# A decoder step on Trainium2: the RWKV triangular solve in 64-column diagonal blocks, merged with its preparation, without padded operands

## What is computed

```python
def step(s, inp):                       # s: value x key, 64 x 64
    rt, wt, kt, vt, kkt, at = inp
    sa = jnp.einsum('bhvk,bhk->bhv', s, -kkt)
    s = (s * wt[:, :, None, :] + sa[..., None] * (kkt * at)[:, :, None, :]
         + vt[..., None] * kt[:, :, None, :])
    return s, jnp.einsum('bhvk,bhk->bhv', s, rt)
```

## Time and profile before

| what | value |
|---|---|
| median of 3 runs | 1461.94 us (1459.42 to 1464.79) |
| the profiled execution: its time / its span | 1466.44 us / 1464.6 us |
| TensorE busy | 1351.8 us (92%) |
| VectorE / ScalarE / GpSimd busy | 972.0 / 646.6 / 395.0 us |
| mean granted TensorE clock | 0.951 of full speed |

### The profile page before, as it was taken

The page is one execution under the profiler, slowest core; times in us unless marked ns, Lnnn a source line. Parts: engine busy times, 40 slices in busy tenths (PEclk is TensorE's granted clock), DMA queues, the critical chain, the costliest instruction groups (busy, mean ns, idle before and its releaser), DMA issues.

```text
span 1464.6 us, 24455 instructions
## 1 busy us (share of the span) xinstructions
PE 1351.8 (92%) x8950; PEld 1177.1 (80%) x8950; DVE 972.0 (66%) x1820; ACT 646.6 (44%) x1492; POOL 395.0 (27%) x316
## 2 busy tenths in 40 slices
PE   6999865898879699999999999999999999799997
PEld 5988642687644499999999999999998778688886
DVE  4566689643543432999802777777776778688887
ACT  4432124332010345444455656656655555455554
POOL 1020113001010003879876000000014777222220
PEclk9999666999969899999999999999999999999999
DMA  6431110000032343555455444344346899889993
GB/s 227 136 115 58 65 74 2 1 2 30 2 126 88 119 128 108 161 150 158 146 171 152 127 130 127 123 130 129 123 136 208 286 300 314 296 300 310 309 320 103
DMA packets 117615, 219.32 MB, mean 150 GB/s; under 512 B 31648, under 2 KB 32160, under 8 KB 116512
## 3 DMA queue, kind: packets, MB, share of 16 engines
q1 hardware_dynamic: 87840, 180.58, 36.8%
q0 software_dynamic: 11264, 33.60, 7.6%
q10 hardware_dynamic: 18432, 4.20, 1.3%
HBM read 207.64 MB, written 10.42 MB: 149 GB/s over the span
## 4 chain that ended last, share of the span: by engine, by line
PE 53%; DMA 5%; POOL 3%; DVE 2%; ACT 2%; issue 1%; SPq 0%; ACTq 0%
PE ph L1720 10%; PE ph L1721 10%; PE ph L1722 10%; PE acc L1787 6%; PE acc L1789 6%; PE acc L1788 6%; PE pg L1768 4%; DMA raw<-in_v 3%; POOL lo L1593 3%; ACT hi L1623 1%; DVE lo L1802 1%; DMA raw<-in_uT 1%; DMA raw<-in_w_q 1%; DMA hid<-in_v 1%; PE acc L1740 1%
## 5 line engine op out<-in xcount | busy, mean ns | idle before, releaser
L1720 PE MATMUL ph<-xh,hi 128*128 128x320 f32 x1152 | 363.7, 316 | 9.5 <-DVE lo L1802 7.0
L1721 PE MATMUL ph<-xl,hi 128*128 128x320 f32 x1152 | 356.5, 309 | 0.0
L1722 PE MATMUL ph<-xh,lo 128*128 128x320 f32 x1152 | 356.4, 309 | 0.0
L1802 DVE TENSOR_TENSOR lo<-raw,hi 128x512 fp32r<-128x512 f32 x328 | 220.2, 690 | 143.9 <-ACT hi L1623 140.5
L1623 ACT ACTIVATE hi<-raw 128x512 fp32r<-128x512 f32 x456 | 268.7, 628 | 100.0 <-DMA raw<-in_uT 33.6
L1720 PEld LDWEIGHTS ph<-xh,hi 128*128 128x128 f32 x1152 | 217.0, 188 | 13.4 <-DVE lo L1802 7.3
L1721 PEld LDWEIGHTS ph<-xl,hi 128*128 128x128 f32 x1152 | 217.1, 188 | 0.0
L1722 PEld LDWEIGHTS ph<-xh,lo 128*128 128x128 f32 x1152 | 216.7, 188 | 0.0
L1593 POOL TENSOR_TENSOR lo<-raw,hi 128x512 fp32r<-128x512 f32 x128 | 186.7, 1482 | 103.5 <-ACT hi L1623 102.8
L1787 PE MATMUL acc<-hi,ch 128*128 128x512 f32 x512 | 201.4, 393 | 12.3 <-DVE cl L1937 12.1
L1788 PE MATMUL acc<-hi,cl 128*128 128x512 f32 x512 | 200.3, 391 | 0.0
(11 more groups left out here) (362 smaller groups left out, 1981.3 us busy)
## 6 DMA issues: line engine op xcount, KB each, us to landing
raw<-in_uT SPq DMA_DIRECT2D x256, 256.0 KB, 2.9
raw<-in_v SPq DMA_DIRECT2D x168, 256.0 KB, 4.3
hid<-in_v SPq DMA_DIRECT2D x88, 256.0 KB, 5.2
wraw<-in_w_in SPq DMA_DIRECT2D x30, 512.0 KB, 3.3
raw<-in_w_q SPq DMA_DIRECT2D x32, 256.0 KB, 3.0
wo<-in_w_out SPq DMA_DIRECT2D x4, 1024.0 KB, 10.8
h_scratch<-act_s ACTq DMA_DIRECT2D x128, 32.0 KB, 1.5
sth<-in_state_h SPq DMA_DIRECT2D x1, 2048.0 KB, 7.7
```

The source lines that it names most:

```text
L1720: pe.matmul(o, hi[s][:, k], xh[:, c], start=begin, stop=False)
L1721: pe.matmul(o, hi[s][:, k], xl[:, c], start=False, stop=False)
L1722: ins = pe.matmul(o, lo[s][:, k], xh[:, c], start=False, stop=end)
L1802: dve.tensor_tensor(wide(lo[n % RING]), raw_at(n)[0], wide(hi[n % RING]), ALU.subtract).then_inc(lo_v, 1)
```

## The change

- The preparation and the solve become one block. Bonus and the transposes of `Bh` and `Kh`, which stood in the preparation, are placed between solve steps on TensorE, ScalarE and VectorE. Their exponential goes to a tensor of its own, `kx`.
- `ARx` becomes `AR` with two parts, A and r times decay; a product for one head reads 64 rows. Nothing is zeroed in the preparation and GpSimd has no instruction in it: the `r` product goes to VectorE, the shift copies to ScalarE. The low-rank products of line 770 read 64 rows each.
- Tiles 0 and 1 keep only the diagonal blocks: all matrices are 128 x 8 x 64, the first chunk of a tile in rows 0 to 63 and the second in rows 64 to 127. Scores are products of 64 rows and 64 columns, four quadrants in turn, with one PSUM bank for each row group. A solve step is 16 products, both chunks in one bank. The masks are packed to this form.
- The three tiles advance together: step s of tile 0, of tile 1, and step s - 2 of tile 2. PSUM is a ring of six banks.
- In the recurrence operands are 64 rows; the state `st` holds both heads of a pair side by side with zeros between, so that four products of 128 rows replace eight; parts that need no state are issued ahead; the sample states are read in 64-row products, scaled by 32 ScalarE instructions, and V is spread for all heads at the start of the block by GpSimd.

Its core, with new functions; masks and additions of the other tiles follow the same pattern, and `y_local`, `s_local`, `u_all`, `s_new`, `y_new` are eight products of 64 rows each, `y_state` four of 128, `carried` one of 512 columns:

```diff
-(M_ID, M_BU, M_BL, M_EU, M_SU, M_IU, M_TBU, M_TBL, M_TIU, M_HI, M_HO, M_B64) = range(NMASK)
+NMASK = 10
+(M_ID, M_BB, M_ES, M_II, M_TBU, M_TBL, M_TIU, M_HI, M_HO, M_B64) = range(NMASK)
...
+    row, left = s % 64, t < 64
+    side = t % 64
+    near = row // 16 == side // 16
+    m[:, M_BB] = near & np.where(left, row < side, row > side)
+    m[:, M_ES] = (row < side) & (~near | ~left)
+    m[:, M_II] = np.where(left, row <= side, row == side)
...
-        ARx = y_mem.sb("ARx", [P, 4, 4, C])
+        AR = y_mem.sb("AR", [P, 4, 2, C])
         Bt = y_mem.sb("Bt", [P, 4, C])
         Kt = y_mem.sb("Kt", [P, 4, C])
         pinc = y_mem.sb("pinc", [P, 4, C])
         vr = y_mem.sb("vr", [P, 3, 512])
-
-        bk = y_mem.sb("bk", [P, 2, 5, 512])
+        bk = y_mem.sb("bk", [P, 2, 3, 512])
...
+        TT = zflat[:, 0:1024].rearrange("p (i h s) -> p i h s", i=2, h=HB)
+        TT2 = heads(zflat[0:w2, 1024:1024 + HB * w2], w2)
+        Et = zflat[:, 1792:2816].rearrange("p (i h s) -> p i h s", i=2, h=HB)
...
+        STEP6 = [("N2", "pwt", "pw", "qwt"), ("N2t", "pw", "pwt", "qw"), ("R1", "qwt", "TT", "TT"),
+                 ("N4", "qw", "qwt", "pw"), ("N4t", "qwt", "qw", "pwt"), ("R2", "pw", "TT", "TT"),
+                 ("N8", "pwt", "pw", "qwt"), ("R3", "qwt", "TT", "TT"),
+                 ("R", "TT", "ident", "qw"), ("F", "Et", "qw", "pwt"), ("Ft", "qw", "Et", "pw"),
+                 ("Z1", "pwt", "TT", "TT"), ("F2", "pw", "pwt", "qwt"), ("Z2", "qwt", "TT", "TT")]
+        NEEDS = {"N2": [], "N2t": [], "R1": ["N2"], "N4": ["N2", "N2t"], "N4t": ["N2", "N2t"], "R2": ["N4", "R1"],
+                 "N8": ["N4", "N4t"], "R3": ["N8", "R2"], "R": ["R3"], "F": ["R"], "Ft": ["R"], "Z1": ["F", "R3"],
+                 "F2": ["F", "Ft"], "Z2": ["F2", "Z1"]}
+        SUMS = {"R1": "tt", "R2": "R1", "R3": "R2", "Z1": "R3", "Z2": "Z1"}
+        NSC = [6, 6, 10]
+        halves = lambda i: (0, 1) if i == 2 else (0,)
+
+        def stage6(s):
+
+            return [(s, i) for i in (0, 1)] + ([(s - 2, 2)] if 2 <= s < 10 else [])
...
-            @block.gpsimd
-            def _(pool):
-                pool.memset(lo_in[0:64, 1], 0.0).then_inc(zeroed, 1)
-                pool.wait_ge(zeroed, 1)
-                pool.memset(lo_in[64:128, 0], 0.0).then_inc(zeroed, 1)
-                pool.memset(ARx[64:128, :, 0::2], 0.0).then_inc(zeroed, 1)
-                pool.wait_ge(zeroed, 3)
-                pool.memset(ARx[0:64, :, 1::2], 0.0).then_inc(zeroed, 1)
-                pool.wait_ge(zeroed, 4)
-                pool.memset(bk[:], 0.0).then_inc(zeroed, 1)
-                pool.memset(vr[:], 0.0).then_inc(zeroed, 1)
-                pool.tensor_copy(sh_out[:, :, 0:1], zbT[:, :, PROMPT:PROMPT + 1]).then_inc(sh_done, 1)
-                pool.tensor_copy(sh_out[:, :, 1:1 + NS], samp(zbT)[:, :, :, 8]).then_inc(sh_done, 1)
-                pool.wait_ge(exps, 1)
-                for g in range(2):
-                    half = slice(64 * g, 64 * g + 64)
-                    if g:
-                        pool.wait_ge(rt_made, 1)
-                    pool.tensor_tensor(ARx[half, :, 2 + g], zm[half, 0:4], pinc[half], ALU.mult).then_inc(rt_made, 1)
...
-                    pe.matmul(psl[:, i, 0:C], lora[:, 0, P * i:P * i + P], lo_in[:, 0], start=True, stop=True)
-                    pe.matmul(psl[:, 4 + i, 0:C], lora[:, 0, P * i:P * i + P], lo_in[:, 1], start=True,
+                    pe.matmul(psl[:, i, 0:C], lora[0:64, 0, P * i:P * i + P], lo_in[0:64], start=True, stop=True)
+                    pe.matmul(psl[:, 4 + i, 0:C], lora[64:128, 0, P * i:P * i + P], lo_in[64:128], start=True,
...
+                def claim(key):
+                    e = at6[key]
+                    if e >= RING6:
+                        pe.wait_ge(*left6[e - RING6])
+                    return psl[:, e % RING6]
+
+                def scores(i):
+                    half = lambda g: slice(64 * g, 64 * g + 64)
+                    if i < 2:
+                        for kind in range(2):
+                            banks = [claim(("sc", i, 2 * kind + g)).rearrange("p (j a t) -> p j a t", j=4, a=2) for g in range(2)]
+                            for j in range(4):
+                                for g, c in ((0, 0), (1, 1), (0, 1), (1, 0)):
+                                    ts = slice(P * i + 64 * c, P * i + 64 * c + 64)
+                                    ins = pe.matmul(banks[g][half(c), j], (Bt, Kt)[kind][half(g), j, ts],
+                                                    AR[half(g), j, :, ts], start=True, stop=True)
+                            ins.then_inc(sc_full, 1)
+                        banks = [claim(("sc", i, 4 + g))[:, 0:256].rearrange("p (j t) -> p j t", j=4) for g in range(2)]
...
+                def solve(s, i):
+                    name, lhs, rhs, _ = STEP6[s]
+                    for q in halves(i):
+                        bank = claim((name, i, q))
+                        if name in ("N2", "N2t"):
+                            pe.wait_ge(sc_free, sum(NSC[:i + 1]))
+                        for r in NEEDS[name]:
+                            pe.wait_ge(*taken[r, i, q])
+                        if name == "R1":
+                            pe.wait_ge(tt_first, i + 1)
+                        a = work(i, lhs)
+                        if i == 2:
+                            view = bank[0:w2, 0:4 * w2].rearrange("p (m t) -> p m t", m=4)
+                            for m in range(4):
+                                h = 4 * q + m
+                                ins = pe.matmul(view[:, m], a[:, h], work(i, rhs)[:, h], start=True, stop=True)
+                        else:
+                            view = heads(bank, 64)
+                            for h in range(HB):
+                                for rows in (slice(0, 64), slice(64, 128)):
+                                    b = ident[rows, rows] if name == "R" else work(i, rhs)[rows, h]
+                                    ins = pe.matmul(view[rows, h], a[rows, h], b, start=True, stop=True)
+                        ins.then_inc(mm_full, 1)
...
+                pe.wait_ge(ar_ready, 1)
+                scores(0)
+                scores(1)
+                for s in range(2):
+                    for step, i in stage6(s):
+                        solve(step, i)
+                scores(2)
+                for s in range(2, 14):
+                    for step, i in stage6(s):
+                        solve(step, i)
+                    if s in (3, 4):
+                        pe.wait_ge(rk_ready, 1)
+                        for i in (2 * s - 6, 2 * s - 5):
+                            if i >= 2:
+                                pe.wait_ge(rk_used, i - 1)
+                            pe.matmul(psl[:, 6 + i % 2, 0:C], masks[:, M_B64], bonusT[:, i], start=True,
+                                      stop=True).then_inc(rk_full, 1)
+                    if 6 <= s < 12:
+                        n = s - 3
+                        what, i = divmod(n, 3)
+                        pe.wait_ge(tok_src, what)
+                        if n < 5:
+                            pe.wait_ge(rk_used, n)
+                        else:
+                            pe.wait_ge(tok_free, n - 1)
+                        src = (Bh, Kh)[what - 1]
+                        for j in range(4):
+                            ins = pe.transpose(psl[0:TW[i], 7 - n % 2, P * j:P * j + P], src[:, j, P * i:P * i + TW[i]], ident[:])
+                        ins.then_inc(tok_full, 1)
...
+                act.activation(sh_out[:, :, 0:1], zbT[:, :, PROMPT:PROMPT + 1], ACT.Copy).then_inc(sh_done, 1)
+                act.activation(sh_out[:, :, 1:1 + NS], samp(zbT)[:, :, :, 8], ACT.Copy).then_inc(sh_done, 1)
...
+                dve.wait_ge(exps, 1)
+                dve.tensor_tensor(AR[:, :, 1], r, pinc[:], ALU.mult)
...
+                dve.scalar_tensor_tensor(out=AR[:, :, 0], in0=At[:], scalar=-1.0, in1=kkn[:], op0=ALU.mult, op1=ALU.mult)
+                dve.tensor_tensor(Kt[:], k7[:], Bt[:], ALU.mult)
...
+                link(dve.tensor_tensor(Bt[:], tmpa[:], Bt[:], ALU.mult))
+                dve.sem_inc(ar_ready, 1)
...
+                masked(0)
+                masked(1)
+                dve.tensor_tensor(bonusT[:], bonusT[:], k7[:], ALU.mult).then_inc(rk_ready, 1)
+                masked(2)
+                for s in range(2, 14):
+                    for step, i in stage6(s):
+                        add_up(step, i)
+                    if s == 3:
+                        dve.tensor_tensor(Bh[:], tmpa[:], kx[:], ALU.mult).then_inc(tok_src, 1)
+                    if s in (3, 4):
+                        for i in (2 * s - 6, 2 * s - 5):
+                            dve.wait_ge(rk_full, i + 1)
+                            dve.tensor_tensor(bonusT[:, i], psl[:, 6 + i % 2, 0:C], v[:, i], ALU.mult).then_inc(rk_used, 1)
+                    if s == 6:
+                        dve.tensor_tensor(Kh[:], k7[:], kx[:], ALU.mult).then_inc(tok_src, 1)
```

(50 more changed lines are left out.)

569 lines of the change are left out of this document (271 added, 298 removed).

## The result

The changed kernel takes 1403.49 us (median of 4 executions, 1401.03 to 1409.77) beside 1461.84 for the kernel before on the same chip: ratio 0.962, 95% interval 0.958 to 0.966, faster. The forecast was 1396, range 1384 to 1430. The profiled execution took 1409.77, span 1407.9, and 56.7 less than the 1464.6 of before; its three edited stages account for 56.5: preparation 33.0 (52.1 before), solve 62.6 (94.0), recurrence 59.9 (65.9). Forecast were savings of 18.5, 32.1 and 15.0. The first two came (19.1 and 31.4); of the third 6.0 came.

What follows compares the result with a forecast made beforehand. VectorE was taken to limit the preparation, TensorE the solve and the recurrence's chunk loop. Savings of 18.5, 32.1 and 15.0, together 65.6, took the profiled 1466.44 to 1400.8; the median, 4.5 lower, gave 1396 us, range 1384 to 1430.

Steps and rivals of the forecast that it cites:

- Preparation, 18.5: Preparation: emptying GpSimd's queue, overlapping low-rank products and moving work into the solve save 18.5 us (bounds 10 and 20).
- The four operations: Preparation after line 883: only four operations of 1408 elements, 6.6 us, remain before the scores; saves 9.1.
- (d): Rival, preparation: GpSimd doesn't cause VectorE's long instructions and low-rank products don't overlap; 1404 us, within the forecast's 0.55 chance.
- Solve, 32.1: Solve: 61.9 us instead of 94.0 with smaller overlapping products and masks, so 32.1 saved.
- The first part: Solve: the part VectorE sets, from scores through the third tile's masks and first product, takes 21.8 us.
- (c): Rival, first score to last chunk: TensorE runs at 1.2 GHz throughout, 76 us more, 1472; chance 0.03.
- Recurrence, 15.0: Recurrence: 51 us against 65.9 with fewer, unpadded products and a shorter end, so 15.0 saved.
- the sum's 51.1: Recurrence: predicted total, 50 us plus 1 for a shorter stall, given as 51.
- rival (b): Recurrence: the clock falls to 1.2 GHz as often one quarter of the array works; +34 us, 1430; chance 0.12.
- 32 ScalarE scalings ... 7.0, after Y (1.5): Recurrence's end: 32 scalings of 64 elements at 0.218 us each take 7.0, following Y's 1.5, on the longest path.
- stand behind U: Recurrence's end: the 128 small passes come after the U product in TensorE's queue; no time was given for them.
- the longest path changes hands: Recurrence behind VectorE's spreading: ScalarE's scalings and additions set the end, 11.5 to 12 us; TensorE's part ends at 8.5.

Runs made afterwards that it cites:

- e1: Changed kernel with GpSimd's old load put back into the preparation (nine memsets, two products into an unused buffer); 1412.86 us.
- e13: Changed kernel with the third tile's scores issued right behind the second's, ahead of the first two steps of tiles 0 and 1; 1406.43 us.
- e3: Changed kernel with the 64 state reads at the recurrence's end cut into 128 products of 32 output columns; 1395.45 us.
- e5: Changed kernel with ScalarE scaling two of four j ahead of the copy of Y and VectorE the other two by broadcast products; 1399.21 us.
- e9: Changed kernel with the next chunk's local X product (last chunk: one carried product) ahead of the U product; 1391.14 us.
- e4: Changed kernel with five unread 512-column filling products, one before each chunk's U product and one ahead of the state reads; 1401.30 us.
- e12: Changed kernel with the new chunk order and 32-column state reads, all behind the last U product; 1394.42 us.
- e2: Changed kernel with each solve step's products for rows and columns 0 to 63 all before those for 64 to 127; 1424.54 us.

## Why the prediction held, and where it was off

- **Preparation, 18.5: right (19.1), and for its reasons.** Lines 870 and 873 gave the 5.9. Line 859's 3.5 came as 3.9: the sigmoids end 2.2 us earlier by the overlapping pairs, and VectorE, no longer slowed, is there before them. The four operations are there. First scores at 247.80 (forecast near 248). (d) falls with e1 and with the pairs of lines 824 and 825.
- **Solve, 32.1: right (31.4).** A tile step is 1.00 instead of 0.90, a step of three tiles 3.45 as forecast (3.98 with its transposes). The wait before the third tile's masks is 3.18 instead of 1.3; where the clock stayed up it was 1.63. The first part came out 1.7 longer than the sum, the second 1.0 shorter. From 263.2 on the granted clock is 1.00, so (c) falls. No run takes out the merged block or the order of the three tiles alone, so how much of the 31.4 each brought is not shown.
- **Recurrence, 15.0: the mechanism right, the size wrong (6.0).** Against the sum's 51.1: first part 5.9 instead of 9.5 (-3.6); three chunks 26.6 instead of 22.5 (+4.1), of which the chunk's work is right (22.0 with its waits, e1 and e13) and the rest is the clock, a small piece of rival (b); from the last chunk to the spreading 8.6 instead of 6.1 (+2.5), again mostly at 0.50; from there to the end 18.8 instead of 12 (+6.8), less the 1 set aside for a stall. Together +8.8. That it was not more is luck: the forecast took a low clock in the first part, and this profile had none there, where e1, e2 and e13 had one and took 8.0 to 8.9.
- **The term that was wrong** is "32 ScalarE scalings ... 7.0, after Y (1.5)". The 128 small passes were seen to "stand behind U" and were given no price, as if VectorE's spreading hid them. But Y stands behind them in TensorE's queue and the scalings behind Y, so they lie on the path: they ended 6.3 us after the spreading began. And rows 7 were no guide to their price, since the change also widened their tile from 32 to 64 columns (e3). The scalings themselves took 7.7 and Y 1.5, as forecast. Of "the longest path changes hands" only half was true: TensorE's products ended 1.2 us behind ScalarE (e5). VectorE's "5.7" for a chunk is not what its listed terms add up to (6.6, with two copies of 0.69); with the one copy of X that the trace shows it took 5.8, and was not the limit.
- **Rival (b)** was real in kind and smaller in size: 4.6 us in the chunks. Behind them 15.9 of 27.4 us were at 0.50; what that cost there was not separated. It was not 34, for the whole recurrence came out 9 above the forecast.

## What to carry to other kernels

When a batch of small products is moved past another in an engine's queue, price it anew with its new tile shape, and follow who stands behind it; that VectorE is busy meanwhile hides nothing for the next product. Fill TensorE's waits with work that is due later anyway (e9: a change of order in the queue, 0.8 to 5.4 us off the chunks): seven of the fifteen waits in these chunks had a spell at half clock right behind them, and e4 and e9 to e12, without such waits, had none there. When two runs of the same code differ by 1.5 us, look at the clock of the stretch before looking for a cause in the code. Before shortening a chain, look for a second one that ends within a microsecond of it.

## What the runs showed of the hardware

- Tiles of 64x64 on the two diagonal quarters overlap while writing different partitions of one PSUM bank: 31 ns a pass of 64 columns in turn, 53 one after the other (e2).
- Passes of 8 columns cost 54.7 ns with 64x64 tiles in two quarters, 13.5 with 64x32 tiles in four places, at much the same granted clock (e3), although there are twice as many. The Trainium skill (TensorE: Matmul & The Clock Gate, LDWEIGHTS) gives a load as its columns divided by 1.2 in ns, 53 for 64 columns and 27 for 32: an estimate that the first fits, with two tiles in turn, and whose second is twice what was measured, with four in turn. No run separates the columns of the load from the number of tiles in turn.
- GpSimd stretched VectorE's instructions by form: four tensor_scalars beside memsets from 1.33 to 5.37 us, a product of two operands beside the same memsets not at all (the row below), a subtraction of two operands beside a GpSimd product from 0.28 to 2.62. The Trainium skill has this distinction (SBUF — State Buffer, Who interferes with whom): two inputs contend only with a GpSimd instruction that reads, a tensor_scalar can take the shared pair by itself. The trace agrees on all three.

```profile
218.16 1.63 DVE L1018 TENSOR_TENSOR tmpa<-kkn 128x1408 f32<-128x1408 f32 x1
```
